# Moving twelve pre-computed weight sums from VectorE to GpSimd in a one-core hybrid decoder block

## The reference, cut to what matters

```python
h = _rmsnorm(x, ln1_w)                       # x: 256 tokens x 2048
proj = h @ w_in                              # gdn qkv, z, a, b, swa qkv, two gates
o_a = _gdn_branch(...)                       # causal conv, gated delta rule, 8 heads
o_b = _swa_branch(...)                       # rmsnorm + rope on q, k; dilated window attention, 12 heads
mixed = sigmoid(gate_a) * (o_a @ w_gdn_proj) + sigmoid(gate_b) * (o_b @ w_swa_proj)
x = x + mixed @ w_out
h = _rmsnorm(x, ln2_w)
u = relu(h @ w_ff1)                          # 2048 -> 8192
x = x + square(u) @ w_ff2                    # 8192 -> 2048
```

## Time and profile before

| | |
|---|---|
| device time, median of 3 | 1511.63 us (1511.16 to 1511.88) |
| span of the profiled execution | 1509.3 us (2.3 us under that median; the page lists no other time of its own) |
| granted TensorE clock | 0.999 of full speed |
| PE busy | 1501.0 us (99%) |
| DVE busy | 1110.1 us (74%) |
| ACT busy | 797.8 us (53%) |
| POOL busy | 94.7 us (6%) |
| transfers | 310.74 MB, mean 206 GB/s |

### The profile page before, as it was taken

The page is one execution under the profiler, slowest core; times in us unless marked ns, Lnnn a source line. Parts: engine busy times, 40 slices in busy tenths (PEclk is TensorE's granted clock), DMA queues, the critical chain, the costliest instruction groups (busy, mean ns, idle before and its releaser), DMA issues.

```text
span 1509.3 us, 19446 instructions
## 1 busy us (share of the span) xinstructions
PE 1501.0 (99%) x7484; PEld 1265.2 (84%) x7484; DVE 1110.1 (74%) x1318; ACT 797.8 (53%) x900; POOL 94.7 (6%) x129
## 2 busy tenths in 40 slices
PE   9999999999999999999999999999999999999999
PEld 7888888888888888888888888888888888888887
DVE  6878756878776877776655566688977566679988
ACT  6554444676654544554444545455545444456654
POOL 5000000000040100100000101100000111110000
PEclk9999999999999999999999999999999999999999
DMA  8578897744545444445755655656566666566873
GB/s 290 201 263 291 306 355 261 242 146 166 169 166 167 140 139 142 140 159 172 250 178 185 195 184 184 189 195 218 176 216 198 196 189 186 185 221 235 301 290 147
DMA packets 150086, 310.74 MB, mean 206 GB/s; under 512 B 7680, under 2 KB 8192, under 8 KB 148224
## 3 DMA queue, kind: packets, MB, share of 16 engines
q1 hardware_dynamic: 148752, 307.65, 61.1%
q10 hardware_dynamic: 1264, 2.13, 0.4%
HBM read 295.09 MB, written 14.68 MB: 205 GB/s over the span
## 4 chain that ended last, share of the span: by engine, by line
PE 92%; DVE 4%; DMA 2%; issue 1%; ACT 1%; SPq 0%; DVEq 0%; ACTq 0%
PE banks L564 42%; PE banks L922 16%; PE banks L990 11%; PE banks L968 9%; PE banks L925 8%; PE banks L580 2%; DVE lo L1474 1%; DMA early_sum<-in_w_ff 1%; DVE lo L2085 1%; PE banks L828 1%; DMA raw<-in_w_ff 1%; PE banks L703 1%; PE banks L676 1%; DVE diag L1493 1%; PE banks L819 1%
## 5 line engine op out<-in xcount | busy, mean ns | idle before, releaser
L1474 DVE TENSOR_TENSOR lo<-raw,hi 128x1024 fp32r<-128x1024 f32 x384 | 473.5, 1238 | 283.8 <-ACT hi L1023 281.4
L1023 ACT ACTIVATE hi<-raw 128x1024 fp32r<-128x1024 f32 x383 | 404.8, 1059 | 436.8 <-PE banks L564 261.0
L564 PE MATMUL banks<-hi,st 128*128 128x512 f32 x1600 | 504.3, 396 | 1.3 <-DVE gates L1818 1.1
L564 PEld LDWEIGHTS banks<-hi,st 128*128 128x128 f32 x1600 | 292.4, 188 | 58.1 <-DVE gates L1818 1.4
L922 PE MATMUL banks<-st,hi 128*128 128x512 f32 x1024 | 321.6, 395 | 0.0
L564 PE MATMUL banks<-lo,st 128*128 128x512 f32 x800 | 312.2, 390 | 0.0
L925 PEld LDWEIGHTS banks<-st,lo 128*128 128x128 f32 x1024 | 192.4, 188 | 45.4
L1424 ACT ACTIVATE hi<-raw 128x1024 fp32r<-128x1024 f32 x136 | 144.2, 1061 | 122.6 <-PE banks L990 88.8
L925 PE MATMUL banks<-st,lo 128*128 128x256 f32 x1024 | 201.2, 278 | 0.0
L2085 DVE TENSOR_TENSOR lo<-raw,hi 128x1024 fp32r<-128x1024 f32 x136 | 165.0, 1221 | 33.5 <-ACT hi L1424 28.2
L564 PEld LDWEIGHTS banks<-lo,st 128*128 128x128 f32 x800 | 150.2, 188 | 32.2
(11 more groups left out here) (296 smaller groups left out, 1632.2 us busy)
## 6 DMA issues: line engine op xcount, KB each, us to landing
raw<-in_w_ff SPq DMA_DIRECT2D x122, 1024.0 KB, 5.2
raw<-in_w_in SPq DMA_DIRECT2D x99, 1024.0 KB, 5.0
raw<-in_w_out SPq DMA_DIRECT2D x16, 1024.0 KB, 5.1
early_sum<-in_w_ff SPq DMA_DIRECT2D x12, 1024.0 KB, 7.2
w_sums<-early_sum SPq DMA_DIRECT2D x12, 1024.0 KB, 9.4
raw<-w_sums SPq DMA_DIRECT2D x12, 1024.0 KB, 5.8
raw<-in_w_gdn_proj SPq DMA_DIRECT2D x8, 1024.0 KB, 5.2
raw<-in_w_swa_proj SPq DMA_DIRECT2D x4, 1024.0 KB, 5.2
```

The costliest lines, as they stand in the source:

```text
L564: last = pe.matmul(acc[:, t], w[:, k0 + 2 * m + kk, P * t:P * t + P], v[:, (i + more) % PIECES, kk, :], start=m == 0 and kk == 0 and a == ...
L1023: act.activation(hi[:, (i + more) % PIECES], raw[:, i // 2 % RAW, 2 * (i % 2):2 * (i % 2) + 2, :], ACT.Copy)\
L1474: dve.tensor_tensor(lo[:, (i + more) % PIECES], raw[:, i // 2 % RAW, 2 * (i % 2):2 * (i % 2) + 2, :], hi[:, (i + more) % PIECES].bitcast(F ...
```

## The change

The three subtractions of each stored sum, the load and the write go from DVE and SP to POOL. POOL starts them when `x_tok` and `x_scr` are no longer read, and works through the twelve without a table: make h, write h out, wait until that write has landed, load h + 2 into the same buffer, go on with h + 1. The differences count on `sum_made`, and `t_made` is left to the local sums. SP's queue holds only the weight tiles there, and DVE's order has no sums. The buffers move from KB 100 and 108 to KB 108 and 116, over the later k and v rows, so the wait for the last writes moves from `b_scaled(0)` to `b_scaled(2)`. `SUM_STEPS` is now the number 12.

```diff
-SUM_STEPS = [20, 28, 36, 44, 51, 56, 61, 66, 71, 76, 81, 86]
-STORED_SUMS = 3 * len(SUM_STEPS)
+SUM_STEPS = 2 * len(STORED_OCTETS)
...
-        early = [sb(f"early_sum{n}", [P, 2, 2 * N], F32, 100 + 8 * n) for n in range(2)]
+        early = [sb(f"early_sum{n}", [P, 2, 2 * N], F32, 108 + 8 * n) for n in range(2)]
...
             for i in range(1, 3):
-                quad_and_sums(2 * i, w_in_v, 0, COL_SWA + N * i)
-                quad_and_sums(2 * i + 1, w_in_v, 0, COL_SWA + SW + N * i)
+                quad(2 * i, w_in_v, 0, COL_SWA + N * i)
+                quad(2 * i + 1, w_in_v, 0, COL_SWA + SW + N * i)
...
+            def sum_in(h):
+
+                half, np_, o = STORED_OCTETS[h // 2]
+                k = 32 * half + 4 * o + h % 2
+                if h >= 2:
+                    pool.wait_ge(ev[f"t_out{h % 2}"], 16 * (h // 2))
+                pool.dma_start(early[h % 2][:], w_2_v[:, k:k + 3:2, span(2 * N * np_, 2 * N)])\
+                    .then_inc(ev[f"t_in{h % 2}"], 16)
+
+            def sum_make(h):
+
+                b = early[h % 2]
+                lower, upper = b[:, 1], b[:, 0].rearrange("p (c n) -> p c n", c=2)
+                pool.wait_ge(ev[f"t_in{h % 2}"], 16 * (h // 2) + 16)
+                pool.tensor_tensor(upper, b[:, :, N:2 * N], upper, ALU.subtract).then_inc(ev["sum_made"], 1)
+                pool.wait_ge(ev["sum_made"], 3 * h + 1)
+                pool.tensor_tensor(lower[:, N:2 * N], lower[:, N:2 * N], b[:, 0, 0:N], ALU.subtract)\
+                    .then_inc(ev["sum_made"], 1)
+                pool.wait_ge(ev["sum_made"], 3 * h + 2)
+                pool.tensor_tensor(lower[:, 0:N], lower[:, 0:N], lower[:, N:2 * N], ALU.subtract)\
+                    .then_inc(ev["sum_made"], 1)
+
+            def sum_out(h):
+                pool.wait_ge(ev["sum_made"], 3 * h + 3)
+                pool.dma_start(w_sums[h // 2, :, :, h % 2, :], early[h % 2][:].rearrange("p r (c n) -> p (r c) n", c=2))\
+                    .then_inc(ev[f"t_out{h % 2}"], 16)
+
+            pool.wait_ge(ev["x_square"], TT)
+            pool.wait_ge(ev["x_split_lo"], KC)
+            sum_in(0)
+            sum_in(1)
+            for h in range(SUM_STEPS):
+                sum_make(h)
+                sum_out(h)
+                if h + 2 < SUM_STEPS:
+                    sum_in(h + 2)
...
-                    if n == 0:
+                    if n == 2:
                         for b in range(2):
-                            dve.wait_ge(ev[f"t_out{b}"], 8 * len(SUM_STEPS))
+                            dve.wait_ge(ev[f"t_out{b}"], 8 * SUM_STEPS)
...
-                ahead(QA + n, 8, steps, more_steps=lambda m, n=n: stored_sums(8 * n + m))
+                ahead(QA + n, 8, steps)
```

More of the change, by code:

```diff
@@ L97 @@
     m_mixed x_back e_turned e_hi e_lo e_square u_made f_first f_copied f_free u_hi u_lo stored c_gate angles ab_act
[L98 removed]
+    ab_vec g_vec n_init s_made s_hi s_lo sum_made t_made t_in0 t_in1 t_out0 t_out1 c_done c_first c_second c_copied""".split()
 def build_block(nc, x, positions, inv_freq, ln1_w, w_in, conv_w, a_log, dt_bias, gdn_norm_w, w_gdn_proj,
@@ L303, in sums_before @@
             before = 2 * len(LOCAL[0]) * half + len(LOCAL[half]) * np_ + LOCAL[half].index(o)
-            return STORED_SUMS + 4 * before
+            return 4 * before
         def source(half, np_, o, n):
@@ L315, in source @@
             return raw[:, t % RAW, k:k + 2, :], landed[t % RAW], 16 * (t // RAW) + 16
-        def sums_now(at, after):
-            return [h for h, step in enumerate(SUM_STEPS) if step + after == at]
         def x1_part(np_, t, j):
@@ L365, in octet_used @@
                     sp.wait_ge(lo_ready, a + 2 * which + 2)
[L367 to L391, removed]
             sp.dma_start(rows[0:KC, 0, :], ln1_w.rearrange("(k p) -> k p", p=P)).then_inc(ev["w_rows"], 16)
@@ L410, in _ @@
             for i in range(1, 3):
-                quad_and_sums(2 * i, w_in_v, 0, COL_SWA + N * i)
-                quad_and_sums(2 * i + 1, w_in_v, 0, COL_SWA + SW + N * i)
+                quad(2 * i, w_in_v, 0, COL_SWA + N * i)
+                quad(2 * i + 1, w_in_v, 0, COL_SWA + SW + N * i)
             for i in range(3):
-                quad_and_sums(QA + 6 + i, w_in_v, 0, COL_SWA + 2 * SW + N * i)
+                quad(QA + 6 + i, w_in_v, 0, COL_SWA + 2 * SW + N * i)
             for i in range(4):
-                quad_and_sums(QB + i, w_in_v, 0, COL_GDN + N * i)
+                quad(QB + i, w_in_v, 0, COL_GDN + N * i)
             with sp.Fori(4, 8) as i:
@@ L437, in _ @@
                         tile(qf, j, w_1_v, 4 * j, FF // 2, first=True)
-                    sp.wait_ge(ev["t_out0"], 8 * len(SUM_STEPS))
-                    sp.wait_ge(ev["t_out1"], 8 * len(SUM_STEPS))
+                    for b in range(2):
+                        sp.wait_ge(ev[f"t_out{b}"], 8 * SUM_STEPS)
                 with sp.Fori(half, 8) as i:
@@ L1529, in right_lo @@
                 return step
[L1531 to L1545, removed]
             def angles():
@@ L1632, in _ @@
                     steps = {}
-                ahead(QA + n, 8, steps, more_steps=lambda m, n=n: stored_sums(8 * n + m))
+                ahead(QA + n, 8, steps)
                 a_post(n % 2, n)
             for i in range(3):
-                ahead(QA + 6 + i, 8, more_steps=lambda m, i=i: stored_sums(8 * (QA + 6 + i) + m))
+                ahead(QA + 6 + i, 8)
             dve.wait_ge(ev["a_turned"], 6)
@@ L1810, in _ @@
                 steps = {m: both(*a) for m, a in steps.items() if a}
-                ahead(QB + gi, 8, steps, more_steps=lambda m, gi=gi: stored_sums(8 * (QB + gi) + m))
+                ahead(QB + gi, 8, steps)
             def gate(q, g, which, i):
```

## The result

The changed kernel takes 1545.26 us (median of 4 runs, 1543.54 to 1546.81) where the kernel before takes 1511.76 in runs on the same chip: a ratio of 1.0222, with an interval of 1.0208 to 1.0237. It is slower, by 33.5 us. The forecast was 1522.4 with a range of 1511 to 1535: the sign and the place are right, the size is a third of the measured one.

The account below looks back on a forecast made before the run. PE was taken to bound the kernel, busy 1501.0 of 1509.3 us. POOL holding DVE in the `a_post` stretches, +11.2 us, less 0.4 us of relief, gave 1511.6 + 10.8 = 1522.4 us, range 1511 to 1535.

Parts of the forecast that it names:

- the tight stretch and its margin: Groups 0 to 5, around each `a_post`: DVE has 9.2 us almost without idle time; delay over 0.9 us delays PE.
- POOL's subtractions, 5.07 us a sum, and the turn of 14 us: On POOL: 2.45 + 2 x 1.31 us per sum; with write, landing and next load, one sum per 14 us.
- the high bound: POOL against DVE in the `a_post` groups: hold 5.9 us, landing 5.2, turn 11.8; loss 3.8 us per group, 23 in all.
- 0.405 of it falls into the tight stretch: `a_post` groups: 9.2 / 22.7 of POOL's 8.2 us hold, 3.33 us, giving 1.86 us loss per group, 11.2 in all.
- The instructions with a scalar don't: On DVE: the reduction and instructions with a scalar don't take the path shared with POOL; only instructions reading two operands do.
- The sums that are left over after 163 us ... nothing there.: Groups 6 to 8, without `a_post`, DVE busy 33.85 of 52 us: POOL's remaining sums there cost nothing.
- Transfers and the moved wait: Closer-packed 24 MB (313 GB/s) and last-write wait moved to the third `gdn_qkv` row block, with 150 us cover: nothing.
- the gain of 0.4 us: DVE without its 31 us of sums and their load waits: PE's stall behind the `early_sum` transfer goes, 0.4 us.
- keep its turn: Rival, `a_post`: DVE's next instruction takes the path before waiting POOL; loss within the margin, 1511.2 us; chance 0.16.
- Slow transfers: Rival: POOL's turns take over 26.8 us, so DVE and PE stand at the moved wait; about 1555 us; chance 0.08.
- Relief: Rival: removing DVE's sums frees PE stalls that the trace hides; faster, about 1508 us; chance 0.06.

Follow-up runs that it names:

- runs with six, three and no tied sums: Changed kernel with six, three or no sums made to start in an `a_post` (DVE's rotary work), the others outside: 1543.56, 1527.04 and 1513.47 us.
- the filler run: Changed kernel plus 13 matmuls with unread products on PE ahead of each of the six waits for the rotated tile: 1534.77 us, ratio 1.0153.
- the memsets: Changed kernel with each sum's three subtractions replaced by three POOL memsets of 128x2048, sums left out: 1519.57 us, ratio 1.0054.
- the late run: Changed kernel with one wait more, so that POOL starts its first sum only after the last `a_post`: 1526.43 us, ratio 1.0104.
- run with copies: Changed kernel with six sums tied to the `a_post` reductions and each subtraction replaced by a same-size copy, sums left out: 1517.79 us, ratio 1.0041.

## Why the prediction was wrong in size

*What bounds the kernel, the tight stretch and its margin.* Right. PE waits at the six transposes and next to nowhere else, and 0.9 us is a fair margin: 4.3 us of hold in group 2 gave 3.3 us of wait.

*POOL's subtractions, 5.07 us a sum, and the turn of 14 us.* Right: 2.38 + 2 x 1.28 = 4.94 undisturbed, and 14.0 beside the rotary work. (By its own row the 2.45 should have been 2.42, and the high bound adds up to a turn of 12.1 us and a loss of 22, not 11.8 and 23.) The landing was 5.4 us (median) where I took 8; POOL's issues were 0.71 to 0.76 us where I took 0.5, and the sums took longer beside DVE.

*"0.405 of it falls into the tight stretch": this step failed.* It kept the stretch at 9.2 us. But a hold makes the stretch longer: with 4.3 us it is 13.5, nearly as long as a turn, and each `a_post` met about one whole sum. I had 2.76 us of hold per group, less the margin 1.86; it is 4.3, and the waits are 22.4 / 6 = 3.7. An estimate from the prediction's own numbers shows how much of the miss this is: POOL holds 2.76 / 9.2 = 0.30 of the stretch, so the hold h follows from h = 0.30 x (9.2 + h), which is 3.9 us, less the margin 3.0, and 18 us in all instead of 11.2. The rest, up to 22.4, goes with the groups having fallen into step with two turns, which an average over phases doesn't see. The runs with six, three and no tied sums show that the price goes by the number of meetings. That the step comes from the turn's length is read from the profile; no run varied the turn alone.

*A term was missing: what PE loses behind a wait.* I took a microsecond of wait for a microsecond of loss. Behind each wait the granted clock went down to 1.2 GHz for a while; the filler run puts this at about 10 us, nearly the size of my whole forecast. A stop costs some 0.5 us beside that. With 22.4 for 11.2, this is the sum: 22.4 + 11.5 = 33.9 us.

*"The instructions with a scalar don't" (take the shared path).* Wrong, as the memsets showed. In the changed kernel it matters in one group, where the sum began late in the `a_post` (72.78 us).

*"The sums that are left over after 163 us ... nothing there."* Nearly right for groups 6 to 8 (1 us in the late run), but only because POOL was done by 194 us. The same argument would have passed the delta branch, where the late run lost 14 us. DVE's busy share said nothing of this.

*Transfers and the moved wait: nothing; the gain of 0.4 us.* Right: 1.0002 with the subtractions back on DVE. The gain is there in every profile, the changed kernel's too: PE's shift against before falls by 0.46 us at 171 us. It is there also where DVE subtracts, so it comes from the earlier load for which DVE no longer waits, and not from DVE's 31 us of relief. No median is good enough to show it.

*The rivals.* DVE doesn't keep its turn: POOL gets in between two multiplies (the pair of 4.59 us at 97.71). Slow transfers: a turn of 14 us, not 26.8. Relief: none.

## What to carry to other kernels

Work given to POOL was not free for DVE here, though POOL was idle: a POOL instruction that read SBUF held DVE's two-operand instructions for its whole length, and one that only wrote held those with a scalar. Before moving it, look for the stretches in which PE waits for DVE's last result, tie POOL's work to the places between them, and where it can't be tied, cut it into short instructions. When you price a wait of PE, let it lengthen the stretch and the group before you average, and add what PE loses behind it, by its clock most of all; here that was another half of the wait.

## What the runs showed of the hardware

- After a wait of PE of some 3 us, eight transposes took 1.97 us instead of 0.87 and the granted clock was 0.50 to 0.79 over 6 to 8 us around such a wait. 3.1 us of useless matmuls in front of each of six waits made the whole kernel about 10 us faster.
- At full clock (1.00, run with copies) a marked wait of PE of 0.53 us made it 1.0 to 1.1 us late.
- A memset on POOL (1.81 us) held a 128x8 instruction of DVE with a scalar for 1.81 us, though that one works for 0.17 us, and left 128x1024 subtractions at 1.22.
- Sixteen short POOL instructions beside DVE make POOL 2.5 times slower (6.04 us against 2.4 for 1024 columns), and the kernel loses a third (11.4 us against 33.0).
